# A top-2 mixture of experts on one core: plain fp32 products on four 32-column tiles in place of three split products

## The reference, cut to what matters

```python
def moe_swiglu(h, w_router, w_gu, w_down):
    t = h.reshape(-1, D)                                   # 256 x 1024
    logits = (t @ w_router).astype(jnp.float32)
    top_val, top_idx = lax.top_k(logits, TOP_K)            # 2 of 8
    top_w = jax.nn.softmax(top_val, axis=-1)
    gates = jnp.sum(jax.nn.one_hot(top_idx, N_EXPERTS) * top_w[..., None], axis=1)
    for e in range(N_EXPERTS):                             # w_gu[e] 1024 x 7168, w_down[e] 3584 x 1024
        out = out + gates[:, e:e + 1] * swiglu(t, w_gu[e], w_down[e])
```

## Time and profile before

| | us |
|---|---|
| runs (3) | 1379.5, 1379.96, 1380.72; median 1379.96 |
| the profiled execution, its own time | 1376.1 |
| its span | 1374.3 |
| TensorE busy | 1344.8 |
| VectorE busy | 1161.9 |
| ScalarE busy | 899.0 |
| mean granted clock of TensorE | 0.994 |

### The profile page before, as it was taken

One profiled execution on the slowest core, in us unless ns is written; L12 is line 12 of the kernel. 1 busy time (PEld: TensorE's weight loads), 2 busy tenths in 40 slices (PEclk: granted clock), 3 DMA queues, 4 the chain that ended last, 5 costly groups with the idle time before them and its releaser, 6 DMA issues.

```text
span 1374.3 us, 19523 instructions
## 1 busy us (share of the span) xinstructions
PE 1344.8 (98%) x6901; PEld 1122.8 (82%) x6901; DVE 1161.9 (85%) x947; ACT 899.0 (65%) x745; POOL 79.5 (6%) x99
## 2 busy tenths in 40 slices
PE   6999999999999999999999999999999999999997
PEld 4599999898778888888888888888888888888885
DVE  6867778788779888888888888888888888898884
ACT  3253433556657777777777777777777777777772
POOL 3500000100210000000000000000000000000001
PEclk9999999999999999999999999999999999999998
DMA  9988999697359999999999999999999999999990
GB/s 362 407 326 310 337 322 339 225 344 298 124 204 374 411 390 351 401 376 379 369 388 385 347 404 382 364 375 389 385 346 403 383 366 382 380 388 351 412 362 33
DMA packets 210250, 476.64 MB, mean 347 GB/s; under 512 B 15040, under 2 KB 38672, under 8 KB 210064
## 3 DMA queue, kind: packets, MB, share of 16 engines
q1 hardware_dynamic: 204928, 457.76, 88.8%
q0 software_dynamic: 5120, 17.86, 4.1%
q10 hardware_dynamic: 144, 0.26, 0.0%
HBM read 466.90 MB, written 10.50 MB: 347 GB/s over the span
## 4 chain that ended last, share of the span: by engine, by line
PE 95%; DVE 2%; ACT 1%; DMA 1%; issue 0%; POOL 0%; SPq 0%; DVEq 0%; POOLq 0%
PE ps L1688 29%; PE ps L1690 29%; PE ps L1689 29%; PE ps L2141 2%; PE ps L1779 1%; DMA raw<-w_mod 1%; DVE wlo L1463 1%; PE ps L1672 1%; PE ps L1768 1%; PE ps L1976 0%; PE ps L2107 0%; PE ps L1706 0%; DVE wlx L1463 0%; PE ps L2065 0%; PE ps L1746 0%
## 5 line engine op out<-in xcount | busy, mean ns | idle before, releaser
L1463 DVE TENSOR_TENSOR wlx<-raw,whx 128x2048 fp32r<-128x2048 f32 x168 | 384.8, 2292 | 97.6 <-ACT whx L983 96.9
L1463 DVE TENSOR_TENSOR wlo<-raw,whi 128x2048 fp32r<-128x2048 f32 x168 | 384.1, 2288 | 4.5 <-ACT whi L983 3.0
L983 ACT ACTIVATE whi<-raw 128x2048 fp32r<-128x2048 f32 x168 | 322.3, 1920 | 88.5 <-PE ps L1690 86.0
L983 ACT ACTIVATE whx<-raw 128x2048 fp32r<-128x2048 f32 x168 | 322.3, 1919 | 84.0 <-PE ps L1690 84.0
L1688 PE MATMUL ps<-whi,thi 128*128 128x512 f32 x516 | 208.0, 403 | 1.5 <-DVE tlo L1106 1.5
L1690 PE MATMUL ps<-whi,tlo 128*128 128x512 f32 x516 | 201.6, 391 | 0.0
L1689 PE MATMUL ps<-wlo,thi 128*128 128x512 f32 x516 | 201.3, 390 | 0.0
L1688 PE MATMUL ps<-whx,thi 128*128 128x512 f32 x460 | 179.9, 391 | 0.5 <-DVE tlo L1435 0.5
L1690 PE MATMUL ps<-whx,tlo 128*128 128x512 f32 x460 | 179.3, 390 | 0.0
L1689 PE MATMUL ps<-wlx,thi 128*128 128x512 f32 x452 | 175.9, 389 | 0.0
L1688 PE MATMUL ps<-thi,whi 128*128 128x256 f32 x480 | 135.9, 283 | 2.1 <-DVE tlo L1106 2.1
(11 more groups left out here) (284 smaller groups left out, 1906.8 us busy)
## 6 DMA issues: line engine op xcount, KB each, us to landing
raw<-moe_w_gu SPq DMA_DIRECT2D x448, 512.0 KB, 5.6
raw<-moe_w_down SPq DMA_DIRECT2D x224, 512.0 KB, 6.2
raw<-w_mod SPq DMA_DIRECT2D x88, 512.0 KB, 5.9
raw<-ffn_w_gu SPq DMA_DIRECT2D x44, 512.0 KB, 5.8
raw<-w_qkv SPq DMA_DIRECT2D x24, 512.0 KB, 5.6
raw<-ffn_w_down SPq DMA_DIRECT2D x22, 512.0 KB, 4.9
shift_w<-w_mod SPq DMA_DIRECT2D x8, 512.0 KB, 16.1
raw<-w_o SPq DMA_DIRECT2D x8, 512.0 KB, 6.4
```

Source lines behind the costliest of these rows:

```text
L983: act.activation(m_hi[m % MRING], raw[:, r % RAW, :], ACT.Copy).then_inc(hi_ready, 1)
L1463: dve.tensor_tensor(m_lo[m % MRING], raw[:, r % RAW, :], m_hi[m % MRING].bitcast(F32), ALU.subtract).then_inc(unit_done, 1)
```

## The change

The stage's products become plain fp32 with no split. The stationary operand is now 32 slots (`g_t[:, k, 32g:32g+32]`), and the array is used as four tiles of 32 columns: tile j writes partitions 32j to 32j+31 of PSUM. Each of the four has its own 256 moving columns of the same weights. 96 slots (`CAP`) are three groups of 32. A chunk of gate and up is laid out so that partition 32j+s holds, for slot s of a group, hidden columns 32j to 32j+31 of each block of 128; VectorE's transpose of 32x32 blocks then gives the activations with the hidden dimension on the partitions.

```diff
-MRING = 6
+RING = 14
+CAP = 96
+ROUNDS = 3
+GROUPS = CAP // 32
...
+        def tile_out(j, b, c0, n):
+            return ps[32 * j:32 * j + 32, b, c0:c0 + n]
...
-                def half_gate_up(c, g, m, e, fresh=False):
-
-                    for kh in range(2):
-                        if fresh:
-                            pe.wait_ge(g_lo, 2 * j0 + kh + 1)
-                        pe.wait_ge(unit_done, r0 + m + 2 * g + kh + 1 + EXPERT_UNITS * e)
-                        sl = (m + 2 * g + kh) % MRING
-                        for kk in range(4):
-                            k, w = 4 * kh + kk, slice(kk * 512, kk * 512 + 512)
-                            mm = three(bank(2 * (c % 2) + g), ghi[:, k, :], glo[:, k, :], m_hi[sl][:, w], m_lo[sl][:, w],
-                                       k == 0, k == KC - 1, False)
+                def loaded(m, e):
+
+                    pe.wait_ge(ring_loaded[m % RING], loads_at(u0 + m) + 32 * (EXPERT_UNITS // RING) * e)
+                    return ring[m % RING]
+
+                def gate_up(c, m, e, fresh=False):
+
+                    for u in range(4):
+                        if fresh and u == 0:
+                            pe.wait_ge(g_hi, j0 + 1)
+                        if fresh and u == 2:
+                            pe.wait_ge(g_lo, j0 + 1)
+                        w = loaded(m + u, e).rearrange("p (i k f j) -> p k i f j", i=2, k=2, f=4)
+                        for kk in range(2):
+                            k = 2 * u + kk
+                            for g in range(GROUPS):
+                                for j in range(4):
+                                    mm = pe.matmul(tile_out(j, 2 * (c % 2) + g // 2, (g % 2) * 256, 256), g_t[:, k, 32 * g:32 * g + 32],
+                                                   w[:, kk, :, :, 32 * j:32 * j + 32], start=(k == 0 and g % 2 == 0), stop=(k == KC - 1),
+                                                   skip_group_check=True)
                         mm.then_inc(unit_used, 1)
 
-                def turn(n):
-                    pe.wait_ge(e_act, n + 1)
-                    for jj in range(4):
-                        mm = pe.transpose(ps[:, 6, jj * P:jj * P + P], actf[:, jj * P:jj * P + P], ident)
-                    mm.then_inc(e_at, 1)
...
+                def down_block(w, c, f, g):
+                    for j in range(4):
+                        mm = pe.matmul(tile_out(j, 4 + g, 0, 256), act_t[c % 4][:, (4 * g + f) * 32:(4 * g + f) * 32 + 32],
+                                       w[:, (f % 2) * D + 256 * j:(f % 2) * D + 256 * j + 256], start=(c == 0 and f == 0),
+                                       stop=(c == NCE - 1 and f == 3), skip_group_check=True)
+                    return mm
```

```diff
+                    dve.wait_ge(e_act, n + 1)
+                    dve.transpose(act_t[c % 4], actf_e).then_inc(e_turned, 1)
```

More of the change, by code:

```diff
@@ L561, in _ @@
             with sp.If(over > 0):
-                experts(1)
+                for ps_no in range(1, ROUNDS):
+                    experts(ps_no)
             rows_out = out[0].rearrange("(t p) d -> p t d", p=P)
@@ L1022, in expert @@
                         m, n = PRE + STEP * c, n0 + NCE * e + c
[L1023 to L1028, removed]
                         if c + 1 < NCE or not last:
-                            silu((c + 1) % NCE, used + 2)
+                            silu((c + 1) % NCE, n + 1, q0 + EXPERT_UNITS * e + m + PRE)
@@ L1038, in expert @@
[L1038 to L1043, removed]
+                            gathered_left(e + j0 + 1)
                     if last or ps_no or not first:
                         act.wait_ge(scattered, 16 * (b0 + e))
-                    if not last:
-                        act.wait_ge(plan_moved, 2 * (b0 + e + 1))
@@ L1059, in experts @@
[L1059 to L1065, removed]
+                    for g in range(GROUPS):
+                        if not last:
+                            act.wait_ge(unit_used, q0 + EXPERT_UNITS * (e + 1) + PRE)
+                        elif g + 1 < GROUPS:
+                            act.wait_ge(y_ps, (GROUPS - 1) * ps_no + g + 1)
+                        else:
+                            act.wait_ge(unit_used, q0 + EXPERT_UNITS * (e + 1))
+                        ins = outputs_left(g)
@@ L1066, in experts @@
+                    ins.then_inc(y_left, 1)
+                gathered_left(j0)
+                silu(0, n0 if ps_no else None, q0 + PRE)
                 expert(0, True, False)
@@ L1567, in expert, with outputs_right @@
+                def outputs_right(g):
+                    for j in range(2, 4):
+                        ins = dve.tensor_copy(y_e[32 * g:32 * g + 32, 256 * j:256 * j + 256], tile_out(j, 4 + g, 0, 256))
+                    return ins
                 def expert(e, first, last):
                     for c in range(NCE):
-                        m, n = PRE + STEP * c, n0 + NCE * e + c
-                        used = q0 + EXPERT_UNITS * e + m
-                        ahead = m + MRING
-                        more = STEP if not last or c + 2 < NCE else (2 if c + 2 == NCE else 0)
@@ L1573, in expert @@
[L1573 to L1578 removed]
+                        n = n0 + NCE * e + c
                         if c == 1 and last:
@@ L1584, in expert @@
                             select(e + 1)
-                        for i in range(1, min(more, PRE)):
-                            expert_low(ps_no, ahead + i, e)
                         if c == 3 and not last:
```

334 lines of the change are left out of this document (164 added, 170 removed).

## The result

The changed kernel takes 1349.94 us (1348.95 to 1351.65, 4 runs) against 1380.34 (1379.5 to 1380.75, 4 runs): a ratio of 0.9782, 95% interval 0.9765 to 0.9799. It is 30 us faster where 59 were forecast; 1350 lies in the range, outside the likeliest case's own. The profiled execution has a span of 1347.1 us against 1374.3.

A forecast was written before the change was run, and what follows sets the result against it. The prediction took TensorE to pace the experts' stage: from the profiled 1376.1 us, 58.2 less for chunks including turns, 0.7 less at the start, 1 more at the end gave 1318; with 3.9 for timed runs, 1321, range 1290 to 1425.

The forecast's parts named there:

- Bound by TensorE, split worth nothing by itself: Experts' stage: TensorE sets the pace; removing ScalarE's copies and VectorE's subtractions of weights, hidden by TensorE, is worth 0.
- Tiles overlap, step 0.219: Stage's products: four column tiles run at once, 0.219 us a step, 0.438 a wave of four, 15.77 a chunk against 16.81.
- Rival C: Stage's products: tiles overlap with a loss, waves of 0.445 to 0.467 us, total 1336 to 1380; chance 0.06.
- D: Each wave on TensorE: weight loads not hidden, 0.66 us a wave, +386 us, total 1766; chance 0.12.
- E: Stage's products: program order lets only neighbours overlap, 0.876 us a wave, +825 us, total 2205; chance 0.08.
- F: Slots: 96 may not hold an expert's tokens, so the stage runs three times, total 3090; chance 0.03.
- Turns: Activations' transposes move from TensorE to VectorE: 0.44 us less per chunk, 24.6 us in all; VectorE's turn is covered.
- Slots: Stage with 96 slots, six waves a unit: products alone gain 0.57 us a chunk; gather and plan about the same, 0.
- Changing between tiles and whole array, taken as 0: TensorE switching between four tiles and the whole array, some 15 times: between 0 and 0.5 us each, taken as 0.
- Ring and transfers: Ring of 14 units: TensorE starts with 14 MB ahead; 399 GB/s needed against 379 now; no wait for weights counted.
- B: Weight transfers bound the stage if 379 GB/s is the ceiling, total 1343; chance 0.11.
- Start and end: Stage's edges: TensorE starts 0.7 us earlier; at the end both scatter halves wait for the last copies, +1 us.

The follow-up runs named there:

- e1: Changed kernel with the middle six experts written out one after another on TensorE instead of a loop; 1310.92 us, ratio 0.9492.
- e6: Changed kernel with each unit's products ordered column tile by column tile instead of one per tile in turn; 2814.86 us, one run.
- e9: As e1, with four transposes of a constant block put back on TensorE ahead of each gate and up product; 1346.4 us, ratio 0.9762.
- e5: As e1, with products for slots 32 to 95 left out after each sum's first step, all weights still moved; 1296.37 us, ratio 0.9401.
- e8: As e1, with 7 units of weights in flight instead of 14; 1330.73 us, ratio 0.965.
- e3: Kernel before the change with two experts in each turn of TensorE's loop; 1383.0 us, ratio 1.0025.
- e4: Kernel before the change with three experts in each turn of TensorE's loop; 1379.57 us, ratio 1.0002.

## Why the prediction was right, and where it was not

*Bound by TensorE, split worth nothing by itself.* Right: 672 large instructions of ScalarE and VectorE are gone, and e1's experts take what its products take.

*Tiles overlap, step 0.219.* Right, and it came from the row of the attention: four tiles cost 0.2166 a step. The chunk was forecast at 15.77 us and measures 15.54. Rival C (a loss from four streams) and D did not come. The rule of the Trainium skill beside D ("TensorE: Matmul & The Clock Gate", "Part 3: Packing small matmuls — row/col tiling"), that a load overlaps products only in another row group, does not hold here: 32-column loads run beside products over all 128 rows, 0.11 us each in the records, without lengthening a step. E did not come in this order, and e6 shows by how little reach. F did not come either: the stage ran once.

*Turns.* Right in sign and cover (transpose 0.58 us, 0.7 taken).

*Slots.* The products gained 0.83 us a chunk where 0.57 was forecast, and this rests on 96 slots as much as on the tiles. A unit took 12 x 0.227 = 2.72 us and takes 6 waves, 2.59. With 128 slots it would be 8 waves, 3.46 us by the same wave (an estimate; no run has it), slower than the split.

*Changing between tiles and whole array, taken as 0.* 0.29 us by e9, inside the bounds; some 15 changes, 4 us, a term that was mis-sized and that the better wave made up for: an expert was forecast at 7 x 15.77 = 110.4 us, gather and plan aside, and takes 110.3 with them.

*Ring and transfers, B.* The ceiling of 379 was wrong as a number, it is 399 to 404, and B was not what made 1350 of 1321, though its 1343 lies nearer than the forecast. An expert needs 111.7 us of transfers in e5 and about 113.7 in e8, so e1 ends on this bound; the 14 units asked for early bridge it.

*Start and end.* The wait of 0.63 us ahead of the stage's first product is gone, as forecast. That this product starts at 405.98, 0.66 earlier, is luck in the number: in the runs of the changed kernel and its variants it starts anywhere from 405.98 to 411.67. The end waits 0.94 (1 forecast).

*The sum: what failed.* It has no term for the supply of instructions. The change makes of some 1100 records of TensorE in the loop's body 4100; the jump back, 0.21 us before and so in none of the rows chosen, became 5.9, of which the queue hides 1.4. With the second stop and the clock's fall a jump costs 8.8 us, five times, 43.8. Taken out (e1) the time is 1310.9; the forecast was 1321, its likeliest case's range 1299 to 1334. The mechanism was right and a cost was missing; that this cost is the body's length is shown by e3 and e4, whose products and ring are the old ones. The prediction's own sign spoke: the granted clock should have stayed at 1.00, and it was 0.98 in the stage.

That 1350 lies inside 1290 to 1425 is luck as far as the cause goes. The range was opened upwards for B, C and D, and none of them brought the 29 us. There is a slip in the sum too: 1318 + 3.9 is 1322, not 1321.

The best version is e1: 0.9492 of the kernel before.

## What to carry to other kernels

Count the instructions of a loop's body before and after a change, not only their durations: cut a product into four and the body can become too long to be kept between turns, and then each jump back stops the engine for as long as its queue doesn't cover. Here 1100 records were kept and 2200 were not; where between them the limit lies was not measured. An idle "issue" at the same line of each turn, and a long branch record there, show it; the cure is a body written out, where the following instructions come in time. Work spread over tiles of the array should be issued to them in turn: the same products tile by tile took 2815 us in place of 1350. And once a stage's engine and its transfers need nearly the same time, read the depth of the ring as a lead that is used up at the difference of the two rates.

## What the runs showed of the hardware

- Four plain fp32 products over 256 columns on four 32-column tiles take 0.432 us, as one does. Over 512 columns a plain product on the whole array takes 2 x 0.428 us, an fp32r product 0.227. So for each 512 columns of weights the split cost 3 x 0.227 = 0.68 us, one plain product on the whole array would cost 0.86, and three groups of 32 slots on the tiles cost one and a half waves, 0.65.
- The jump back over a body of 2200, 3300 or 4100 records lasts 5.2 to 6.3 us with the DMA engines at a share near 1; over 4100 records with a share of 0.21 to 0.26, 3.4 us (median); over 1100 records 0.2 us.
- After stops of 4.7 to 5.1 us the granted clock was at the lower level for 4 to 8 us; after one of 1.7 us, in e3, it stayed at the upper.
- With 12 records on one tile and then 12 on the next, some four records of the next tile start beside the last ones of the tile before; 62 records took 9.21 us, 0.149 each.
- One core drew 404 GB/s from memory over 700 us.
